# First block of a two-block model: the recurrent branch's work moved ahead of the memory softmax, its output merged last, and gate evictions moved ahead of the second index block

## The reference, cut to what matters

```python
y_a = a_b * causal_conv3(a_c * a_x, conv_w)
y_b = dsa_attention(q, k, d_v, iq, ik, iw)      # top-64 keys per query, chosen by an index score
hq = silu(g_q); log_f = log(lb + (1 - lb) * sigmoid(g_f)); hk = 1 - exp(log_f)
y_c = rmsnorm(hgrn2_chunkwise(hq, hk, g_i, log_f), hgrn_out_norm) * silu(g_g)
y_m = softmax(rmsnorm(m_q) @ rmsnorm(mk).T * scale) @ mv
gates = sigmoid(gate_logits)                    # four gates of 1024 columns
merged = sum(gates[n] * (branches[n] @ w_lift[n]) for n in range(4))
x = x + merged @ w_out
```

## Time and profile before

| | |
|---|---|
| median of 3 runs | 2418.09 us (2410.25 to 2418.4) |
| profiled execution | 2413.57 us, span 2411.8 us |
| busy: PE, DVE, ACT | 2223.8 us (92%), 1432.0 (59%), 808.7 (34%) |
| mean granted clock of PE | 0.947 of full speed |
| layer one of the first block up to the output matrix | 0 to about 436 us |
| layer two of it, the stretch that answers to 130 to 368 | about 770 to 1010 us |

### The profile page before, as it was taken

The page is one execution under the profiler, slowest core; times in us unless marked ns, Lnnn a source line. Parts: engine busy times, 40 slices in busy tenths (PEclk is TensorE's granted clock), DMA queues, the critical chain, the costliest instruction groups (busy, mean ns, idle before and its releaser), DMA issues.

```text
span 2411.8 us, 36101 instructions
## 1 busy us (share of the span) xinstructions
PE 2223.8 (92%) x15182; PEld 1903.9 (79%) x15182; DVE 1432.0 (59%) x2371; ACT 808.7 (34%) x1026; POOL 57.5 (2%) x79
## 2 busy tenths in 40 slices
PE   6999879999999987999999989988899989989997
PEld 6987869799898866887997777876499967556996
DVE  4871557599568535576886285574377562634544
ACT  3452532244335445213442262221153312103342
POOL 0000000000000000010000000000100000000000
PEclk9999979999999988899999898998899989999999
DMA  6442336677364322377874122010387433203552
GB/s 225 141 146 100 120 105 243 215 235 236 123 189 148 123 105 105 137 261 248 281 258 131 35 105 71 2 37 1 130 265 233 148 134 105 70 9 122 183 184 70
DMA packets 207767, 348.59 MB, mean 145 GB/s; under 512 B 20643, under 2 KB 111562, under 8 KB 207221
## 3 DMA queue, kind: packets, MB, share of 16 engines
q1 hardware_dynamic: 192704, 290.89, 36.2%
q0 software_dynamic: 14624, 55.31, 6.7%
q10 hardware_dynamic: 276, 0.08, 0.0%
HBM read 345.21 MB, written 1.05 MB: 144 GB/s over the span
## 4 chain that ended last, share of the span: by engine, by line
PE 79%; DVE 13%; ACT 5%; issue 2%; DMA 1%; SPq 0%; DVEq 0%; ACTq 0%
PE psum L442 33%; PE psum L825 28%; PE psum L479 15%; DVE G L1324 2%; DVE wide_room L1324 1%; ACT A L928 1%; DMA ring<-in_w_in_dram 1%; DVE ring_low L1324 1%; PE psum L803 1%; DVE ring_low L1197 1%; DVE tmp L1324 1%; DVE A L1324 1%; PE psum L551 1%; DVE A L1702 1%; PE psum L537 0%
## 5 line engine op out<-in xcount | busy, mean ns | idle before, releaser
L1197 DVE TENSOR_TENSOR ring_low<-ring,high_weights 128x2048 fp32r<-128x2048 f32 x124 | 284.2, 2292 | 144.3 <-ACT high_weights L1190 141.6
L825 PE MATMUL psum<-high_rows,high_weights 128*128 128x256 f32 x1280 | 362.1, 283 | 0.0
L825 PE MATMUL psum<-high_rows,ring_low 128*128 128x256 f32 x1280 | 361.4, 282 | 0.0
L442 PE MATMUL psum<-hT,ring 128*128 128x128 f32 (+1 forms) x1552 | 263.9, 334 | 18.3 <-DVE G L1324 7.1
L479 PE MATMUL psum<-mix_rows_high,ring_low 128*128 128x256 f32 x960 | 273.1, 284 | 0.0
L442 PEld LDWEIGHTS psum<-hT,ring 128*128 128x128 f32 x1552 | 238.1, 202 | 43.2 <-DVE x L1324 7.3
L825 PEld LDWEIGHTS psum<-high_rows,ring_low 128*128 128x128 f32 x1280 | 243.8, 190 | 0.0
L825 PEld LDWEIGHTS psum<-high_rows,high_weights 128*128 128x128 f32 x1280 | 241.5, 189 | 2.5 <-issue 1.2
L1190 ACT ACTIVATE high_weights<-ring 128x2048 fp32r<-128x2048 f32 x124 | 237.9, 1918 | 3.9
L479 PEld LDWEIGHTS psum<-mix_rows_high,ring_low 128*128 128x128 f32 x960 | 185.5, 193 | 0.0
L825 PE MATMUL psum<-x2T_low,high_weights 128*128 128x256 f32 x640 | 180.6, 282 | 0.0
(11 more groups left out here) (441 smaller groups left out, 3834.3 us busy)
## 6 DMA issues: line engine op xcount, KB each, us to landing
ring<-in_w_in_dram SPq DMA_DIRECT2D x36, 2048.0 KB, 7.8
ring<-in_ffn_w_dram SPq DMA_DIRECT2D x66, 1024.0 KB, 5.4
ring<-in_ffn_w_up_dram SPq DMA_DIRECT2D x44, 1024.0 KB, 6.3
A<-in_mod_w_dram POOLq DMA_DIRECT2D x40, 1024.0 KB, 7.5
ring<-in_ffn_w_down_dram SPq DMA_DIRECT2D x22, 1024.0 KB, 5.0
ring<-in_w_lift_dram SPq DMA_DIRECT2D x16, 1024.0 KB, 9.1
ring<-in_ab_w_in_dram SPq DMA_DIRECT2D x7, 2048.0 KB, 8.4
ring<-in_hy_w_in_dram SPq DMA_DIRECT2D x6, 2048.0 KB, 8.1
```

The lines of the kernel that those rows point to most:

```text
L442: return pe.eng.matmul(out, lhsT, rhs, start=(k == 0), stop=(k == n - 1))
L825: ins = pe.eng.matmul(out, lhs[a], rhs[b], start=first and n == 0, stop=last and n == 2)
L1197: v.eng.tensor_tensor(low, whole, high.bitcast(F32), ALU.subtract).then_inc(*v.mark(f"w_lo/{l}.{i}"))
```

## The change

It is the same for both layers of the first block.

1. ACT evicts g_f and g_q before it evicts the second index block (`index_kept(1)`).
2. ACT takes the Ln of the forget gate in place, within the softmax of the first 128 tokens.
3. DVE makes `cum` and the two differences for the states' keys and the inner queries right after the memory branch's norms (before merge (0,2)), and ACT their Exps before the memory exps. DVE's three products that need only these follow the memory maximum. Room 1 and 3 of `work` and part of `A1` hold them.
4. The inner keys' difference (`ke_log`), its Exp (`ke_decay`) and product come when `mpT` has freed `A2`, ahead of merge (1,1) on DVE.
5. On PE the logits of a half come before a merge unit and its outputs behind it; unit (2,0) comes before both turns of y, which have a buffer for each half.
6. The recurrent output becomes the fourth branch and the memory output the third (`BRANCHES`), with the panels to match.
7. DVE makes the low parts of gate 0.1 after `mk_ms` and `mq_ms`.

```diff
-    BRANCH_ROOM = (0, 1, 0, 2)
+    BRANCHES = (0, 1, 3, 2)
+    BRANCH_ROOM = (0, 1, 2, 0)
+    y_rec = (ytok, sq[:, 2:4, :].rearrange("p a t -> p (a t)"))
+    cum_room = work[:, 1, :]
+    to_end = work[:, 3, :]
...
+            for t in range(MT):
+                recurrent_logits(t)
                 merge_unit(l, 1, 2 + t)
-                turn(f"hgrnT_ready/{l}.{t}", lambda i: ytok[:, i * P:(i + 1) * P], 4, [f"y_c/{l}.{t}"])
+                recurrent_outputs(t)
+            merge_unit(l, 2, 0)
+            for t in range(MT):
+                turn(f"hgrnT_ready/{l}.{t}", lambda i: y_rec[t][:, i * P:(i + 1) * P], 4, [f"y_c/{l}.{t}"])
...
+            index_kept(0)
             for u in range(2):
                 prepared(l, "g_f{}", 2 * u + 1)
...
+            index_kept(1)
+
             prepared(l, "g_i{}", 3)
...
+                    a.wait_ge(*reached(f"f/{l}"))
+                    copy(ksT[:, :, :], ksT[:, :, :], f"logf/{l}", func=ACT.Ln)
...
             sigmoid_of(l, 0, 3)
+            a.wait_ge(*reached(f"cum/{l}"))
+            copy(to_end, to_end, func=ACT.Exp)
+            copy(A1[:, 0:1024], A1[:, 0:1024], func=ACT.Exp)
+            copy(A1[:, 1024:2048], cum_room, func=ACT.Exp)
+            copy(top["decay"][:, :], ..., f"decays/{l}", func=ACT.Exp)
...
-            (wait f, Ln, wait cum, five Exp)
+            a.wait_ge(*reached(f"ke_log/{l}"))
+            copy(A2[:, 0:1024], A2[:, 0:1024], f"ke_decay/{l}", func=ACT.Exp)
             sigmoid_of(l, 1, 1)
...
-            lows(l, "gate{}.0.1", 0)
             v.wait_ge(*reached(f"pT/{l}.1.3"))
...
+            lows(l, "gate{}.0.1", 0)
             v.wait_ge(*reached(f"mk_rs0/{l}"))
             (newton, product, root)
+            v.wait_ge(*reached(f"logf/{l}"))
+            v.wait_ge(*reached(f"logits_ready/{l}.1"))
+            for half in range(2):
+                e.tensor_tensor_scan(cum_room[:, cc], consts["chunk_scan"], flat(ksT)[:, cc], 0.0, ALU.mult, ALU.add)
+            tt(part(to_end), at(CHUNK - 1), c3, ALU.subtract)
+            tt(part(A1[:, 0:1024]), c3, at(CHUNK // 2 - 1), ALU.subtract, f"cum/{l}")
             merge(l, 0, 2)
...
+            v.wait_ge(*reached(f"decays/{l}"))
+            v.wait_ge(*reached(f"hq/{l}.1"))
+            tt(flat(ksT), flat(hk), to_end, ALU.mult, f"ksT/{l}")
+            tt(A1[:, 0:1024], A1[:, 0:1024], flat(conv_a), ALU.mult, f"qe/{l}")
+            tt(A1[:, 1024:2048], A1[:, 1024:2048], flat(conv_a), ALU.mult, f"qi/{l}")
...
             merge(l, 1, 0)
-            (wait mem_y, scans, three subtractions, ksT, merge (1,1), ke, qe, qi)
+            tt(part(A2[:, 0:1024]), at(CHUNK // 2 - 1), c3, ALU.subtract, f"ke_log/{l}")
+            v.wait_ge(*reached(f"ke_decay/{l}"))
+            tt(A2[:, 0:1024], A2[:, 0:1024], flat(hk), ALU.mult, f"ke/{l}")
+            merge(l, 1, 1)
...
                 (mask of half t)
+                merge(l, 1, 2 + t)
                 v.wait_ge(*reached(f"o_sq/{l}.{t}"))
                 (root, three products of y)
-                merge(l, 1, 2 + t)
```

More of the change, by code:

```diff
@@ L77 @@
     "hgrn_worked": "ksT ke qe qi state cum f attT o_read",
+    "hgrn_logs": "ke_log",
     "branch_done": "y_aT y_b y_c mem_probs mkT",
@@ L746, in tensor, with recurrent_logits @@
                 ins.then_inc(*pe.mark(label))
-            for t in range(MT):
+            def recurrent_logits(t):
                 label = f"hgrn_att_ready/{l}.{t}"
@@ L1048, in act_program, with index_kept @@
                 copy(qT[:, 2 * u:2 * u + 2, :], b, f"q_raw/{l}.{u}", [f"read d_q_ready/{l}.{u}"], scale=S(l, 92))
-            for t in range(MT):
+            def index_kept(t):
                 W = P * (t + 1)
-                if t:
-                    prepared(l, "g_q{}", 3)
                 b = take(f"index_ready/{l}.{t}")
@@ L1120, in act_program @@
             sigmoid_of(l, 0, 3)
+            a.wait_ge(*reached(f"cum/{l}"))
+            copy(to_end, to_end, func=ACT.Exp)
+            copy(A1[:, 0:1024], A1[:, 0:1024], func=ACT.Exp)
+            copy(A1[:, 1024:2048], cum_room, func=ACT.Exp)
+            copy(top["decay"][:, :], cum_room.rearrange("p (c t) -> p c t", t=CHUNK)[:, :, CHUNK - 1], f"decays/{l}", func=ACT.Exp)
             for t in range(MT):
@@ L1139, in act_program @@
                 label = f"mem_y_ready/{l}.{u}"
-                copy(yT[:, BRANCH_ROOM[3], 2 * u:2 * u + 2, :], take(label).rearrange("p (c t) -> p c t", c=2), f"y_mT/{l}.{u}",
+                copy(yT[:, BRANCH_ROOM[2], 2 * u:2 * u + 2, :], take(label).rearrange("p (c t) -> p c t", c=2), f"y_mT/{l}.{u}",
                      ["read " + label])
[L1143 to L1151, removed]
+            a.wait_ge(*reached(f"ke_log/{l}"))
+            copy(A2[:, 0:1024], A2[:, 0:1024], f"ke_decay/{l}", func=ACT.Exp)
             sigmoid_of(l, 1, 1)
@@ L1162, in act_program @@
                     a.wait_ge(*a.own())
-                sigmoid_of(l, 1, 2 + t)
+            sigmoid_of(l, 2, 0)
+            for t in range(MT):
                 a.wait_ge(*reached(f"lift_ready/{l}.0.3"))
                 label = f"hgrnT_ready/{l}.{t}"
-                copy(yT[:, BRANCH_ROOM[2], :, t * P:(t + 1) * P], take(label).rearrange("p (c t) -> p c t", c=4),
+                copy(yT[:, BRANCH_ROOM[3], :, t * P:(t + 1) * P], take(label).rearrange("p (c t) -> p c t", c=4),
                      f"y_cT/{l}.{t}", ["read " + label])
@@ L1169, in act_program @@
                 for q in range(4):
-                    sigmoid_of(l, n, q)
+                    if (n, q) != (2, 0):
+                        sigmoid_of(l, n, q)
             for t in range(MT):
@@ L1569, in dve_program @@
             merge(l, 1, 0)
[L1571 to L1584, removed]
[L1585 to L1589 removed]
+            for u in range(2):
+                v.wait_ge(*reached(f"mpT_ready/{l}.0.{u}"))
+            tt(part(A2[:, 0:1024]), at(CHUNK // 2 - 1), c3, ALU.subtract, f"ke_log/{l}")
+            v.wait_ge(*reached(f"ke_decay/{l}"))
+            tt(A2[:, 0:1024], A2[:, 0:1024], flat(hk), ALU.mult, f"ke/{l}")
             merge(l, 1, 1)
[L1591 to L1593 removed]
             decay = lambda c: top["decay"][:, :].rearrange("p (h c) -> p h c", h=4)[:, :, c:c + 1].broadcast_to([P, 4, P])
@@ L1762, in source @@
             _, n, half = name.split(".")
-            return [(by_four, rows(io["w_lift"][l, int(n)], int(half) * HALF, HALF))]
+            return [(by_four, rows(io["w_lift"][l, BRANCHES[int(n)]], int(half) * HALF, HALF))]
         if kind == "gate":
             _, n, half = name.split(".")
-            return [(whole, rows(io["w_in"][l], COL["gates"] + int(n) * D + int(half) * HALF, HALF))]
+            return [(whole, rows(io["w_in"][l], COL["gates"] + BRANCHES[int(n)] * D + int(half) * HALF, HALF))]
         if kind == "out":
```

30 lines of the change are left out of this document (15 added, 15 removed).

## The result

The changed kernel takes 2350.36 us (median of 4 runs, 2345.53 to 2351.39), the kernel before beside it 2414.79 us (median of 4, 2410.25 to 2418.4). The ratio is 0.9735, with a 95% interval from 0.9721 to 0.975. The forecast was 2349. The profiled execution took 2350.07 us, with a span of 2348.3.

What follows compares the result with a forecast made beforehand. TensorE (PE), busy 92% of the span, was taken as the bound, losing time to waits and half clock. 7.8 - 1.3 + 26.0 = 32.5 us a layer, 65 for two, from 2413.6 gave 2349 us; range 2341 to 2357.

Steps and rivals of the forecast that it cites:

- Part 1: Gates evicted ahead of the second index block: PE starts g_i without waiting, 7.8 us gained a layer, bounds 5.9 to 8.7.
- Part 2: Memory branch, 240.6 to 300.8: work is added, 1.3 us lost a layer, bounds 0.7 gained to 5.5 lost.
- Part 3: Recurrent branch, 300.8 to unit (2,1): waits removed, small pieces near full clock, 26.0 us gained a layer, bounds 17 and 27.
- item (c): Memory branch: ACT's four Exps precede the memory exps, DVE's three products fill its wait; probs from 282.95 to at most 284.7.
- Rival 1: Recurrent stretch: the clock does not recover, small pieces take 21 us instead of 12.4, total 2371; chance 0.08.
- Rival 4: Slower: ACT waits at its queue's head for panel 2.1 as panels and modulation weights collide, up to 2429; chance 0.03.
- Rival 5: New order doesn't change what PE waits for, DVE's mask waiting behind the low parts: 2414; chance 0.04.
- Rival 2: Memory branch: DVE is the bound, scans and products reach PE in full, 5.5 us lost a layer, 2357; chance 0.13.

Runs made afterwards that it cites:

- the last experiment: Changed kernel with both of gate 0.1's low parts early, scans behind the memory maxima, DVE's two subtractions behind lift (1,0)'s addition: 2329.57 us, ratio 0.966 to the kernel before.
- one low part early: Changed kernel with the low part of gate 0.1's second half made directly behind the memory keys' newton step: 2334.37 us, ratio 0.9676; again 2335.89 us, 0.9684.
- low part first: Changed kernel with gate 0.1's first low parts back ahead of the keys' mean squares: 2350.82 us, ratio 0.9744 to the kernel before.
- second run: The kernel with one low part early, timed once more unchanged: 2335.89 us, ratio 0.9684 to the kernel before.
- both low parts early: The kernel with one low part early, with gate 0.1's first-half low part also ahead of `mq_ms`: 2337.02 us, ratio 0.9685 to the kernel before.
- old evictions: Changed kernel with ACT's old order of evictions, the second index block ahead of the forget gates: 2364.45 us, ratio 0.98 to the kernel before.
- turns together: Changed kernel with both turns of the recurrent result put ahead of unit (2,0): 2361.64 us, ratio 0.9789 to the kernel before.

## Why the prediction was right, and where its sizes were off

The forecast was 2349 us, measured 2350.36; the profiled run was to take 2348.6 and took 2350.07. Parts 1 and 3 were found near their terms, each for the reason given. That the total came within 2 us is in part luck: part 2 cost 3.8 us more in the two layers than said, and part 3 gave 2.4 us more.

- **Part 1**, 7.8 a layer: 7.5 and 8.2. No wait was left between the index block and g_i, which starts at 132.09. The first low part of gate 0.0 was ready at 167.02; with the 0.68 us that the index block was sooner in this run this is 167.7, to the tenth what was said. PE came for it at 167.16, which is 167.84 and not 166.8, so DVE was not late: g_i and g_g took 22.4 us and not 21.5, as the slow clock had cost them 1.9 us and not 2.7. Undone and done alone the part moved the time by 14 to 16 and by 12 to 13 us, in the profiles by 10.8 and 17.8.
- **Part 2**, 1.3 lost a layer: 2.5 and 3.9, within the bounds (5.5 lost) but off by a factor of two to three. This is the term that was mis-sized. In the times of the kernel before, which the prediction used (the changed kernel's plus 8.19), gate (0,2) started at 246.0 (246.2 to 247.6 said), PE came for the fourth block at 260.9 (258.1 to 261.6), the part was ready at 264.4 (264.3), and the wait was 3.51 us in layer 1 and 4.85 in layer 2 (2.7 to 6.2). The memory logits then started 1.2 us late, near the end of the range given. Left out was that the slow clock comes back in a place where there is no new wait: in item (c) the memory outputs, 3.69 us in the kernel before, took 5.38 in both layers, behind pauses of 1.14 and 0.84 us instead of 0.93 and 1.17. That is 1.7 a layer, of which 0.4 came back in the turns ahead of them. In layer 2 the new wait was longer, and the block behind it slower as well (5.40 us against 4.38), so that the memory logits started 2.6 us late there.
- **Part 3**, 26.0 a layer: 27.2 and 27.2. The sum said 40.8 us up to unit (2,1) and the trace has 39.8 (295.15 to 334.97); the 66.8 us that this is taken from are 67.0 in the trace of the kernel before. The three units took 9.21, 9.19 and 9.21, 0.5 more than said. Less these, 0.8 for the turns and 0.3 for `kstok`, 11.1 is left for the small pieces; the term was 12.4, with 11.5 for full clock, at which they all ran. DVE kept up as computed: the first mask was due near 309.4 and came at 302.89, which is 308.5 with the 5.65 us that all comes sooner. In the changed kernel's own times PE asks for it at 308.81, 5.9 us later; the second y is done at 331.68, and PE asks at 334.62.
- **Rival 1** (the clock stays low): the 39.90 us row at 1.00 is against it. Half clock in every small piece was also the worst that a clock falling again and again could do. **Rival 4**: ACT's waits for the weights' DMA total 42.8 us in 8 waits, 46.1 in 8 before, and the longest is 11.5 in both. **Rival 5**: `rot_t` is no longer waited for. (Its price, 2414, was that of no gain at all; the waits for the mask were 14.6 us of it.)
- **Rival 2** (DVE is the bound in the memory branch, 5.5 lost) is half true. Waits for `ring_low` over 3 us were named as its sign, and a wait of 3 to 6 us for a low part also as a sign of being right. Waits of 3.51 and 4.85 us came, and they can't tell one from the other. By size, the 2.5 us lost in layer 1 are nearer the forecast and the 3.9 in layer 2 nearer the rival. What DVE held up was the low part behind the scans and subtractions, as the one line that moves it shows, and not the softmax chain; that chain became the bound once PE came to it sooner.
- The prediction held that a row with pauses of about a microsecond at full clock spoke against a clock falling again in the small pieces. Part 3 came out at full clock but is no test of this, as it had no pause but one of 0.31 us. For the memory outputs it didn't hold: see below.

Not tried: the swap of the two branches alone, whose price was taken as nothing, and the kernel with the decayed keys late again. That the wait of 7.87 us for them went is read from the timeline; what it was worth with the slow work behind it wasn't timed by itself.

## What to carry to other kernels

Price a wait of PE at what it is plus the slow work behind it: here waits of 3 to 6 us, taken away or put in, moved the time up to a later common point by 1.3 to 2.4 times their length, so a low part that was late by 3.5 and 4.9 us was worth 12 to 14 us in two layers, and one line moved it. When work is added to DVE ahead of something that PE asks for, list everything in DVE's order between the added work and that request; two of the misses here were a short instruction that stood behind work of no urgency (the fourth block's low part, 1.2 us, behind two scans and two subtractions; the addition of the lift, 0.7 us, behind two subtractions). And when a wait is removed, look for the next chain at once: the second low part gained nothing on top of the first, nor with the scans out of the chain of the softmax; a gain came only when the subtractions had left that of the lift too.

## What the runs showed that was not expected

After short pauses the clock goes either way. The sixteen matmuls of the memory outputs took 3.69 us after pauses of 0.92 and 1.17 us (the kernel before and the last experiment, both layers of each), and after 1.12 and 0.84 in layer 1 of the kernel with one low part early. In layer 1 of the kernel with the low part first, after the same 1.12 and 0.84, they took 5.38. In layer 2 of the kernel with one low part early, after 0.27, 1.03 and 0.84, they took 5.38 too, and its second run had the same split, 3.69 in layer 1 and 5.38 in layer 2. Its stretches, the first line layer 1 and the second layer 2:

```profile
274.90:278.70 3.80, 3.75 (x18) 3.37 (x19) 0.48 (x1) 0.60 (x1) 0.00 (x0) 1.00 0.00 0
...
877.40:882.90 5.50, 5.44 (x18) 4.55 (x19) 0.49 (x1) 0.60 (x1) 0.00 (x0) 0.69 0.00 0
```

Even a wait of fixed length and place has no fixed price. After 1.95 us at the same point of layer 2, the same 32 matmuls took 6.69 us in the changed kernel, 3.76 in the one with the low part first and 7.06 in the one with both low parts early (in this order):

```profile
820.38 6.69 PE L447 MATMUL psum<-dvw,A 128*128 128x64 f32 x32 [1.95 <-ACT A L944]
```

```profile
824.35 3.76 PE L447 MATMUL psum<-dvw,A 128*128 128x64 f32 x32 [1.95 <-ACT A L944]
```

```profile
819.27 7.06 PE L447 MATMUL psum<-dvw,A 128*128 128x64 f32 x32 [1.95 <-ACT A L944]
```

The pause just ahead of it, before four turns, was 0.62 us in the first and 0.16 in the other two: between these two the pauses are the same, and the price is not.

Nor is a slow stretch always its wait's. The 48 gate matmuls of unit (0,2), 8.63 and 7.29 us after a wait of 1.68 in the changed kernel, still took 7.41 and 7.42 after 0.37 in the last experiment, and 5.89 after 1.68 in layer 2 of the kernel with the old evictions. At full clock they take 5.9. What sets the clock there isn't shown.

So the same order of work can differ by some 3 us at each such wait; that it is the shift of everything by a few microseconds which decides it is a guess. Over a longer stretch it adds up: from PE's wait for `A` (1234.85 us in the changed kernel) to its wait of 8.0 us for `G` (1636.69), with the same work in all kernels, the kernel before takes 404.2 us, the changed one 401.8, the one with the old evictions 399.4 and the one with the turns together 397.3. The kernel with the low part first made up the 3.4 us that it had lost in layer 1 in this way: at the turns ahead of the 32 matmuls of layer 2 it was 4.4 us late, and at the memory sums 1.0 us early. It may be how those with the turns together and with the old evictions gave back 4.5 of 15.3 and 4.6 of 15.4. An effect below some 3 to 5 us a layer can't be read from one profile of this kernel.
